# Grouped sums of squares, turned tiles inside a unit and a split router end, in a two-block network with 64 experts

## The reference

```
x = x + w_out @ mix3(fox(h), delta_rule(h), stick_breaking(h))   h = rmsnorm(x)   # 4 heads of 128
x = x + cross_attention(rmsnorm(x), rmsnorm(mem))                # 256 memory tokens
x = x + w_down @ conv_glu(w_up @ rmsnorm(x))                     # 2816 hidden = 22 chunks of 128
x = x + w_out2 @ [retention(h), gated_conv(h)]                   h = rmsnorm(x)
h = rmsnorm(x); lg = h @ router + bias                           # 8 groups + 64 experts
group = argmax(lg[:8]); two best experts within that group       # first of equals wins
x = x + sum over the 2 experts of gate * down(silu(gate_w h) * up_w h)   # 64 experts, 512 wide
y = rmsnorm(x)
```

## Time and profile before

| | us |
|---|---|
| median of 3 runs | 1644.4 (1643.86 to 1644.59) |
| the profiled execution | 1643.81 |
| its span in the trace | 1642.0 |
| TensorE busy | 1351.0 (82%) |
| VectorE busy | 611.0 (37%) |
| ScalarE busy | 480.2 (29%) |

### The profile page before, as it was taken

The page is one execution under the profiler, slowest core; times in us unless marked ns, Lnnn a source line. Parts: engine busy times, 40 slices in busy tenths (PEclk is TensorE's granted clock), DMA queues, the critical chain, the costliest instruction groups (busy, mean ns, idle before and its releaser), DMA issues.

```text
span 1642.0 us, 32810 instructions
## 1 busy us (share of the span) xinstructions
PE 1351.0 (82%) x14414; PEld 1066.6 (65%) x14414; DVE 611.0 (37%) x996; ACT 480.2 (29%) x800; POOL 0.2 (0%) x4
## 2 busy tenths in 40 slices
PE   9999999999999999998876766676676576668666
PEld 9998899999999999995543433343343343334333
DVE  7956646677877778652101101110010110111001
ACT  6855367455644464431000000000000000000001
POOL 0000000000000000000000000000000000000000
PEclk9999999999999999999997988898898898899879
DMA  8442033553556755499999999999999999999997
GB/s 328 156 153 78 26 129 129 180 183 126 203 192 244 275 197 190 156 377 388 421 429 434 427 432 425 431 433 425 432 427 429 434 428 429 428 429 432 426 432 323
DMA packets 41400, 517.92 MB, mean 315 GB/s; under 512 B 4720, under 2 KB 4848, under 8 KB 6384
## 3 DMA queue, kind: packets, MB, share of 16 engines
q1 hardware_dynamic: 41184, 516.71, 76.8%
q10 hardware_dynamic: 144, 0.17, 0.0%
HBM read 515.81 MB, written 1.05 MB: 315 GB/s over the span
## 4 chain that ended last, share of the span: by engine, by line
PE 52%; DMA 41%; DVE 3%; ACT 2%; issue 1%; SPq 0%; another core or an unknown queue 0%; DVEq 0%; ACTq 0%; PEldq 0%
DMA e_gu<-experts 41%; PE psum L324 11%; PE psum L325 11%; PE psum L326 11%; PE psum L916 7%; PE psum L957 3%; PE psum L388 1%; PE psum L566 1%; PE psum L963 1%; ACT w_high L1030 0%; PE psum L927 0%; DMA all_x<-x_t 0%; PE psum L943 0%; DVE w_low L1587 0%; SPq L2295 0%
## 5 line engine op out<-in xcount | busy, mean ns | idle before, releaser
L916 PE MATMUL psum<-e_gu,x_xt 128*32 128x256 f32 x3072 | 228.5, 464 | 167.8 <-DMA e_gu<-experts 167.7
L916 PEld LDWEIGHTS psum<-e_gu,x_xt 128*32 128x32 f32 x3072 | 112.1, 132 | 276.9 <-DMA e_gu<-experts 178.4
L324 PE MATMUL psum<-h_high,w_high 128*128 128x256 f32 x864 | 245.9, 285 | 0.0
L1587 DVE TENSOR_TENSOR w_low<-w_raw,w_high 128x2048 fp32r<-128x2048 f32 x100 | 228.4, 2289 | 44.8 <-ACT w_high L1030 38.8
L325 PE MATMUL psum<-h_low,w_high 128*128 128x256 f32 x864 | 243.5, 282 | 0.0
L326 PE MATMUL psum<-h_high,w_low 128*128 128x256 f32 x864 | 243.4, 282 | 0.0
L1030 ACT ACTIVATE w_high<-w_raw 128x2048 fp32r<-128x2048 f32 x100 | 191.2, 1915 | 66.2 <-PE psum L326 54.7
L2261 DVE COPY x_yb<-psum 128x256 f32<-128x256 f32 x64 | 27.2, 425 | 419.7 <-PE psum L957 419.7
L324 PEld LDWEIGHTS psum<-h_high,w_high 128*128 128x128 f32 x864 | 163.7, 189 | 5.7 <-issue 3.8
L325 PEld LDWEIGHTS psum<-h_low,w_high 128*128 128x128 f32 x864 | 163.7, 189 | 0.1
L326 PEld LDWEIGHTS psum<-h_high,w_low 128*128 128x128 f32 x864 | 163.6, 189 | 0.0
(11 more groups left out here) (453 smaller groups left out, 2132.1 us busy)
## 6 DMA issues: line engine op xcount, KB each, us to landing
e_gu<-experts SPq DMA_DIRECT2D x44, 4096.0 KB, 52.9
w_raw<-dense SPq DMA_DIRECT2D x100, 1024.0 KB, 4.8
e_dn<-experts SPq DMA_DIRECT2D x46, 2048.0 KB, 49.2
e_dn<-experts SPq DMA_DIRECT2D x36, 1024.0 KB, 54.8
e_gu_lo<-experts SPq DMA_DIRECT2D x16, 2048.0 KB, 51.5
e_gu_hi<-experts SPq DMA_DIRECT2D x16, 2048.0 KB, 55.9
e_gu<-experts SPq DMA_DIRECT2D x8, 1024.0 KB, 8.5
e_gu<-experts SPq DMA_DIRECT2D x2, 2560.0 KB, 10.5
```

What stands on the lines that cost most here:

```text
L324: mm(ps, w[0], src[0], start=start, stop=False, **kw)
L916: last = mm(half(psum[32 * s:32 * s + 32, GU_BANK[j % 2], 0:256], P), X["xt"][:, k, CAP * j:CAP * (j + 1)], expert_gu(j, k)[:, :, s * P:(s ...
L1587: V.tensor_tensor(low(w), raw[:, place(w), :], high(w).bitcast(F32), ALU.subtract).then_inc(sem("w_low"), 1)
```

## The change

- `mean_square` goes. `group_sums` has the 8 matmuls 32 columns wide and puts them into four column groups of the array; ScalarE copies the four partial sums out (`keep_sums`), one matmul adds them (`total`), and the root follows (`mean_root`). The unit's products stand between the two where there are any.
- The memory tokens are loaded earlier into a place of their own, squared, summed and normalised ahead of the residuals of `out0`. `U0` is computed chunk by chunk.
- The 16 turns go between the halves of `sk0`; the sums of the fox heads' norm get another tile than `sq`, `lm(0)` goes ahead of the fox norm, and `sb_evac(2)` behind the first evacuation of the inverse's solver.
- The `spread` of the retention norm goes from the middle of `u21` to its end.
- The router's chain is rewritten: ranks by comparing all pairs of 8, over both token halves at once. Only the four experts of the first pass are placed at first.
- `keep_x` consists of transposes in two halves. The first gather runs in four pairs of chunks, between quarters of the first expert's gate and up.
- `o211` has another layout, so that its slot is reloaded in halves; the down half of expert 2 and the two halves of `gu3_hi` wait for less. Behind the first four quarters the gate and up of expert 5 is loaded ahead of the down of expert 4.

```diff
-            def mean_square(name, first=0, last=DC):
-                ps = aux.fill(pe, f"ms_{name}") if first == 0 else psum[:, 4 + aux.units[f"ms_{name}"] % 4, :]
-                for k in range(first, last):
+            def group_sums(name, sq=sq):
+                ps = aux.fill(pe, f"ms_{name}")
+                for k in range(DC):
                     pe.wait_ge(sem("squares"), quarter(name, k // 2))
-                    ins = mm(ps[:, 0:T], C("inv1024"), sq[:, k, :], start=(k == 0), stop=(k == DC - 1))
+                    g = 32 * (k % 4)
+                    ins = mm(ps[g:g + 32, 0:T], C("ones", n=32), sq[:, k, :], start=(k < 4), stop=(k >= 4))
+                ins.then_inc(sem("group_sums"), 1)
+            def total(name):
+                pe.wait_ge(sem("group_sums_kept"), NORMS.index(name) + 1)
+                ps = psum[:, aux.banks[aux.units[f"ms_{name}"] % len(aux.banks)], :]
+                aux.filled(mm(ps[:, T:2 * T], C("ones", n=P), sq[:, 1, :], start=True, stop=True), f"ms_{name}")
...
-            mean_square("mix")
+            group_sums("mix")
+            total("mix")
...
-            unit("sk0")
-            for t in range(TT):
+            def turns():
+                for t in range(TT):
...
+            unit("sk0", between=turns)
...
-            mean_square("mem")
             unit("out10", mixed); unit("out11", mixed)
-            unit("mk0", hm, split_input("mem"))
-            mean_square("xq")
+            unit("mk0", hm, split_input("mem"), between=lambda: group_sums("xq"))
+            total("xq")
...
-                    if c == 0 and g == 0:
-                        mean_square("ffn")
+                    if c == 0 and (k, g) == (DC - 1, 0):
+                        group_sums("ffn")
...
+                if c == 0:
+                    total("ffn")
...
-            mean_square("n1")
-            unit("q21", r_gained)
+            group_sums("n1")
+            unit("q21", r_gained, between=lambda: total("n1"))
...
-            unit("u21", between=lambda: spread("rv", sq[:, 0, :], T))
+            unit("u21")
+            spread("rv", sq[:, 0, :], T)
...
+            pe.wait_ge(sem("htok"), 2)
+            keep_x(bank_of["htok00"], bank_of["htok10"])
             pe.wait_ge(sem("htok"), 4)
-            keep_x(0, 1, 2, 3)
+            keep_x(bank_of["htok01"], bank_of["htok11"])
...
+            def gather_pair(q):
+                gather(2 * q, 4 + q % 2, 0)
+                gather(2 * q + 1, 4 + q % 2, 1).then_inc(sem("xt_lo" if q < 2 else "xt_hi"), 1)
...
+                    if first and k % 2 == 0:
+                        if k:
+                            gather_pair(k // 2 + 1) if k < DC - 2 else None
+                        pe.wait_ge(sem("xt_lo_kept" if k < DC // 2 else "xt_hi_kept"), k // 2 % 2 + 1)
...
+            def ahead_of(out, values):
+                pairs = X["sg"][:, :, 0:64].rearrange("p t (a b) -> p t a b", b=8)
+                other = values.rearrange("p t (a b) -> p t a b", a=1).broadcast_to([P, TT, 8, 8])
+                own = values.rearrange("p t (a b) -> p t a b", b=1).broadcast_to([P, TT, 8, 8])
+                link(V.tensor_tensor(pairs, other, own, ALU.subtract))
+                outranks = C("outranks").rearrange("p (t a b) -> p t a b", t=1, b=8).broadcast_to([P, TT, 8, 8])
+                link(V.tensor_tensor(pairs, pairs, outranks, ALU.is_ge))
+                link(V.tensor_reduce(out, pairs, AX, ALU.add))
...
-            normalise("n1", x, R["cat"], "norm1", H_PARTS)
+            normalise("n1", x, R["cat"], "norm1", H_PARTS, meanwhile="k21")
...
-            sp.wait_ge(sem("down"), 1)
-            load_down(GROUP, 0)
-            for j in range(1, GROUP):
+            sp.wait_ge(sem("gate_up"), GROUP + 1)
+            load_gate_up(GROUP + 1, 1)
+            for j in range(2):
+                sp.wait_ge(sem("down"), j + 1)
+                load_down(GROUP + j, j)
+            for j in range(2, GROUP):
```

More of the change, by code:

```diff
@@ L857, in _ @@
             token_squares(2, 3)
-            w = parts("o211", DC)
+            parts("o211", DC)
+            w = [v.rearrange("p (i k n) -> p i k n", i=2, k=DC) for v in (high("o211"), low("o211"))]
             for i in range(2):
@@ L924, in group_pass @@
                 pe.wait_ge(sem("placed"), i + 1)
[L925 to L932 removed]
+                if first:
+                    gather_pair(0)
+                    gather_pair(1)
+                    aux.wait_empty(pe, "rank")
+                else:
+                    for c in range(DC):
+                        last = gather(c, 4 + c // 4, c % 4)
+                        if c == 3:
+                            last.then_inc(sem("xt_lo"), 1)
+                    last.then_inc(sem("xt_hi"), 1)
+                    pe.wait_ge(sem("xt_lo_kept"), i + 2)
                 gate_up(i, 0, first)
@@ L1013, in high_parts, with gained_high @@
                     ac(dst[:, 2 * q:2 * q + 2, :], src[:, 2 * q:2 * q + 2, :], ACT.Copy).then_inc(sem("input_high"), 1)
-            def gained_high(name, src, ready, gain, dst):
+            def gained_high(name, src, ready, gain, dst, meanwhile=None):
                 for k in range(DC):
+                    if k == DC - 2 and meanwhile:
+                        ahead(meanwhile)
                     if k % 2 == 0:
@@ L1050, in _ @@
             squares("mix", x, lambda q: (sem(f"x_loaded{q // 2}"), 16))
-            ahead(UNITS[0], 2)
+            ahead(UNITS[0], 1)
+            keep_sums("mix")
             act.wait_ge(sem("consts_loaded"), 16)
-            root("ms_mix", sq[:, 0, :])
+            mean_root("mix")
             ahead(UNITS[0], 3)
@@ L1148, in sb_evac @@
                 if u == 0:
-                    root("fss_sum", sq[:, 0:2, :], 512)
+                    root("fss_sum", half(A["tmp"]), 512)
                 ahead(f"{nm}{u % 2}")
@@ L1273, in _ @@
             gates("c", 1, 0); gates("c", 1, 1)
-            for hf in range(2):
-                for p in range(2):
-                    gates("b", hf, p)
-            ahead("ob_1")
-            act.wait_ge(sem("mixed"), 4)
-            squares("mem", M["mem"], lambda q: (sem("mem_loaded"), 16))
+            ahead("oc_1")
+            gates("b", 0, 0); gates("b", 0, 1)
+            act.wait_ge(*done["oc_1"])
+            squares("mem", mem_raw, lambda q: (sem("mem_loaded"), 16), mem_sq)
+            gates("b", 1, 0)
+            keep_sums("mem")
+            gates("b", 1, 1)
+            warm(ACT.Sqrt)
+            mean_root("mem")
             ahead("out00")
-            warm(ACT.Sqrt)
-            root("ms_mem", sq[:, 0, :])
-            ahead("out01")
             high_parts("mem", M["mem"], hm[0])
@@ L1347, in _ @@
             ahead("mo_0")
-            gained_high("ffn", x, added(1), "norm_ffn", f_gained[0])
+            gained_high("ffn", x, added(1), "norm_ffn", f_gained[0], meanwhile="mo_1")
             squares("ffn", x, added(1))
-            ahead("mo_1")
             warm(ACT.Sqrt)
-            root("ms_ffn", sq[:, 0, :])
+            keep_sums("ffn")
+            mean_root("ffn")
             ahead("U0")
@@ L2201, in places @@
+            aux.release(dve, "rank")
             def places(g0):
```

294 lines of the change are left out of this document (161 added, 133 removed).

## The result

The changed kernel takes 1630.8 us (median of 4 runs, 1629.04 to 1631.45), the kernel before 1644.1 in the same comparison (1643.78 to 1644.59). The ratio is 0.9917 with a 95% interval of 0.9900 to 0.9934: faster by 13.4 us, where 18.9 was forecast. The profiled execution takes 1630.11 us with a span of 1628.2, which is 13.8 us less than before. One execution in what follows, of x1 (1787.1 us at a mean granted clock of 0.735), was a slow one and is left out of its comparison.

A forecast was written before the change was run, and what follows sets the result against it. TensorE bounds the kernel until about 745 us, then a fixed-rate expert load stream that starts with the first release. Norms 7.9, turns 5.8, spread 0.8 and router's end 4.4 sum to 18.9 us: 1625.5 us, range 1620.5 to 1632.5.

The forecast's parts named there:

- Rival A: TensorE's clock falls during the wait for `D0`, perhaps also between router logits and gather: 1627.2 to 1630.5 us, chance 0.25.
- rival B: Shorter norms leave VectorE and ScalarE too little time for following units' parts: 6.3 us lost, 1629 to 1633, chance 0.12.
- The turns: Delta rule's decay sums: turns half a unit earlier remove the 3.19 us wait and half clock; 5.8 us, bounds 3.2 to 6.1.
- The norms: Grouped sums replace `mean_square`: `mix` 1.3, `mem`, `xq` and `n1` 2.1 us each, `ffn` 0.3; together 7.9 us.
- The FFN's term: `ffn` norm: saving mostly becomes a wait of about 2.5 us at `D0` for `w_low`; 0.3 us gained, bounds 0 to 2.1.
- The half clock: Cost of a stretch at half clock behind a TensorE wait, as priced in Rival A: between 1.7 and 2.9 us.
- spread: Moving the retention norm's spread to the end of `u21` removes a wait for VectorE; 0.8 us, bounds 0 to 0.8.
- The router's chain and the rank: Router's end: VectorE's rewritten chain brings `x_member` 2.45 us earlier, the rank step 0.13; gather starts 2.6 us earlier.
- whatever brings that release forward by 1 us brings the end forward by 1 us: Start of expert stream: release of expert 0's first quarter sets the end one for one, if earlier loads are in.
- the last term: First gather to first release of expert 0's slot: 3.05 us instead of 4.88, so 1.8 us less.
- this sign: Profile sign: first release to end stays 894.8 us as before; if it moves, the stream is not what was thought.
- rival D: Load queue decides the release: late halves wait for something later, 4.4 us lost, 1629.9 us, chance 0.04.

The follow-up runs named there:

- x1: The kernel before, with 13 idle matmuls inside TensorE's wait of 3.19 us at the decay sums (L549); median 1643.1 us, ratio 0.9995.
- x11: The changed kernel with ScalarE's `sb_evac(2)` ahead of the key scaling again, the turns still inside `sk0`; 1636.4 us.
- x10: The changed kernel with the turns behind `sk0` again, ScalarE's order as changed; 1629.9 us.
- x4: The changed kernel with the first down unit behind the fifth up unit, whose low part is made ahead of the taps; 1630.0 us.
- x12: The changed kernel with x3's idle matmuls, first gather in halves, x4's unit order, and low parts of the sixth and seventh up units earlier too; 1624.1 us, ratio 0.9876.
- x7: The changed kernel with x3's idle matmuls and the first gather whole ahead of the first expert's gate and up; 1629.6 us.
- x5: The changed kernel run and profiled again, with no edit; median 1628.4 us.
- x3: The changed kernel with 6 idle matmuls inside the wait for the member matrix, ahead of the first gather; 1627.9 us, ratio 0.9902.
- x2: The changed kernel with 8 idle matmuls inside the wait for the first down unit's low part; 1628.1 us.
- x9: The changed kernel with the idle matmuls of both x2 and x3; 1628.2 us.

## Why the prediction was right, and where not

The measured time lies in the range (1620.5 to 1632.5), 5.3 us above the point and above the forecast of 1624 to 1627. Rival A, the half clock behind the wait for `D0` and again ahead of the gather (1627.2 to 1630.5, chance 0.25), is what the first profile shows, at both places; in it the stream lost 1.7 us besides. By its number alone 1630.8 lies in the stretch that went to rival B, whose mechanism did not come: behind the other norms TensorE waits for no low part of a unit. That the range held is in part luck, since the measured time contains a loss in the stream that the prediction had put at nothing.

**The turns** (5.8 forecast, 5.9 found) were right in size and in both parts: x1 puts the half clock at 2.3 us in the trace (2.6 by the prediction), and x11 brings the wait and the half clock back. The prediction gave the gain to the turns' place, half a unit earlier; x10 shows that ScalarE's order carries all but 1.6 us of it.

**The norms** were right in kind and a little high. `mem` and `xq` gave 3.7 and not 4.2, `n1` 1.9 and not 2.1: the grouped sums, with the slower product behind them, take 1.20 us in the chain, the upper end of the bounds, and not 0.95. The prediction's sentence on the Trainium skill ("TensorEngine Tiling (Array Packing)", Key Properties: changing the tiling mode drains TensorE) gave 1.9 for each norm, by a loss paid twice. The trace agrees with its 1.9 better than with the 2.1 that I used, but the chain shows the extra 0.20 us behind the sums alone, and none behind the total. `mix` gave 0.8 and not 1.3: TensorE waited 0.51 us for the copy, but the sums also began 0.16 us later, and no other work stood behind either part. The FFN's term was right in its reason (the saving turns into a wait at the down unit, 2.2 us where 2.5 was forecast) and gave 0.7 and not 0.3. x4 and x12 show that this wait was one of order in VectorE's list: with the down unit later alone it moves on, with the low parts in the order of need it goes.

**The half clock** was priced at 1.7 to 2.9 us and cost 1.2 at the down unit and 1.4 in the gather. No row shows the 1.7, and the earlier trace rows show 2.6 (half of 5.26) and not 2.9. That it comes in some executions only was not forecast. Rival A weighed the new wait against the idle time from 182.5 us on, which had kept the clock; in x7, x10 and x12 the same place lost it, so this one row of before could not tell the two apart. The half clock accounts for 2.6 of the 5.2 us that the first profiled execution stands above its forecast (1630.11 against 1624.9).

**The router's chain and the rank** were right (2.4 and 0.2 against 2.45 and 0.13).

**The step that failed** is "whatever brings that release forward by 1 us brings the end forward by 1 us, as long as the earlier loads are in by then". Its condition was wrong: I had those loads in 3.4 us ahead of the release (739.4 in the frame of before, which is some 725 in x5), and they landed at 730.3, 1.6 us behind it. Even in the kernel before, the load issued at 739.55 landed at 747.56, 0.3 us behind the release. What was left of these loads is small, though, 0.2 us of stream. The larger part is that the stream needs all four quarters in time, not the first: released 2.1 us apart they leave a hole, which halves shrink and a whole gather avoids, and more of the later loads comes before the first long one is complete. A release that moves with its whole train does move the end, as x3 shows (1.3 us of 1.4). From the start of the gather to the end of the long load the pairs gain nothing against before (91.85 and 91.78 us), and 0.8 us against the whole gather of x7 (92.63). So the 1.8 us of the last term were lost whole: in x5, with full clock, the release came 18.5 us earlier than before and the end 16.6. The prediction had named this sign: from the release to the end it expected 894.8 us, and 896.5 and 896.7 were found. Of rival D, in which the loads and not the release decide and 4.4 us are lost, this is a small part.

In sum, for x5: 18.9 forecast, less 1.8 for the stream and 1.2 for the norms (`mix` 0.5, `mem`, `xq` and `n1` 0.7), more 0.4 for the FFN and 0.2 for turns and spread, makes 16.5; found are 16.6, with 0.4 of it from an earlier start, so that 0.3 us stay unexplained.

## What to carry to other kernels

When a stage is bound by a stream of loads, look at the whole train of first releases and at when the loads ahead of it land, not at the first release alone: here 1.8 us of earlier first release bought nothing over the old kernel, and in the traces 0.7 us once the second release came close behind it. A list of work on a helping engine can leave the engine that it feeds waiting while being far from full; moving the consumer only moves the wait, and putting the list in the order of need removes it (x4 and x12). A wait of 2 us can cost more than its length, here up to 1.4 us, though not in every execution; to price it from one profile is to take one draw. Idle matmuls in such a wait did no harm here, but no median shows that they gain.

## What the runs showed of the hardware

- One and the same program, with the same wait of 2.19 us, lost TensorE's clock in one execution and kept it in another (granted clock 0.57 and 1.00 over 433 to 437 us). Waits of 3.19 and 4.93 us were both followed by half clock. The Trainium skill ("TensorE: Matmul & The Clock Gate", What's actually happening) says that activity releases the throttle; the fillers of x1, x2, x3 and x9 agree as far as they go, since none of the waits that they filled was followed by half clock, while five of the thirteen unfilled ones at the down unit and the gather were.
- Executions of these programs differ by up to 1.5 us by the first norm already (the `mix` sums begin between 15.64 and 17.15 us). The three late ones (x3, x4, x9) had half clock over 11 to 14 us, behind a wait of 2.3 to 2.4 us.
- Loads of 1 MB released 2.1 us apart on a stream that moves 1 MB in 2.4 us did not keep it full: 270 GB/s over two microseconds, at a DMA share of 0.97, against 418 when they came 0.9 us apart.
